# Decoder layer on one core: order of weight splits in the late up chunks, residual rows in two loads, one load later in block 0

## The reference, cut to what matters

```python
x = x + jnp.concatenate([y_mix, y_mem], axis=-1) @ w_out      # (2048, 1536) @ (1536, 1024)
h = rms_norm(x, norm_mlp)
u = jax.nn.relu(h @ w_up)                                     # (2048, 1024) @ (1024, 4096)
x = x + (u * u) @ w_down                                      # (2048, 4096) @ (4096, 1024)
return rms_norm(x, final_norm)
```

## Time and profile before

| what | value |
|---|---|
| median of 3 runs | 2483.25 us (2482.57 to 2483.95) |
| the profiled execution: its own time | 2490.13 us |
| its span, first to last instruction | 2488.3 us |
| PE busy | 2459.6 us (99%) |
| DVE busy | 1869.7 us (75%) |
| ACT busy | 1350.0 us (54%) |
| POOL busy | 344.0 us (14%) |
| mean granted TensorE clock | 0.999 |
| DMA | 411.69 MB, 165 GB/s on the mean |

### The profile page before, as it was taken

One profiled execution on the slowest core, in us unless ns is written; L12 is line 12 of the kernel. 1 busy time (PEld: TensorE's weight loads), 2 busy tenths in 40 slices (PEclk: granted clock), 3 DMA queues, 4 the chain that ended last, 5 costly groups with the idle time before them and its releaser, 6 DMA issues.

```text
span 2488.3 us, 34865 instructions
## 1 busy us (share of the span) xinstructions
PE 2459.6 (99%) x13020; PEld 2125.0 (85%) x13020; DVE 1869.7 (75%) x2779; ACT 1350.0 (54%) x2060; POOL 344.0 (14%) x328
## 2 busy tenths in 40 slices
PE   7999999999999999999999999999999999999998
PEld 7888888888788888888978888898888888889987
DVE  5677468778867887878766778877785677887777
ACT  5544354544554456556655445665565445556655
POOL 0044200000303320000020441000020143000000
PEclk9999999999999999999999999999999999999999
DMA  8422458777842143566552216355664212545555
GB/s 295 169 68 68 163 192 301 256 271 254 281 167 68 52 171 125 174 207 211 199 174 77 76 51 203 110 195 195 210 211 139 84 60 80 192 142 180 186 176 180
DMA packets 236741, 411.69 MB, mean 165 GB/s; under 512 B 10304, under 2 KB 142784, under 8 KB 227616
## 3 DMA queue, kind: packets, MB, share of 16 engines
q1 hardware_dynamic: 235952, 409.20, 48.3%
q10 hardware_dynamic: 624, 0.27, 0.0%
HBM read 365.39 MB, written 44.04 MB: 165 GB/s over the span
## 4 chain that ended last, share of the span: by engine, by line
PE 91%; DVE 4%; DMA 2%; issue 2%; ACT 1%; ACTq 0%; DVEq 0%; POOLq 0%; POOL 0%; SPq 0%
PE banks L2690 27%; PE banks L2692 26%; PE banks L2691 26%; PE banks L2865 3%; DMA raw<-w_mix 1%; DVE w_lo L2497 1%; PE banks L2844 1%; PE banks L2904 1%; PE banks L2908 1%; PE banks L2889 1%; PE banks L2821 1%; DVE u_lo L2408 1%; PE banks L2834 1%; PE banks L2920 1%; DVE c_parts L2541 1%
## 5 line engine op out<-in xcount | busy, mean ns | idle before, releaser
L2690 PE MATMUL banks<-h_hi,w_hi 128*128 128x512 f32 (+1 forms) x1728 | 606.0, 351 | 1.6 <-DVE h_lo L2300 0.7
L2692 PE MATMUL banks<-h_hi,w_lo 128*128 128x512 f32 (+1 forms) x1728 | 598.5, 346 | 0.0
L2691 PE MATMUL banks<-h_lo,w_hi 128*128 128x512 f32 (+1 forms) x1728 | 598.5, 346 | 0.0
L2497 DVE TENSOR_TENSOR w_lo<-raw,w_hi 128x1024 fp32r<-128x1024 f32 (+1 forms) x312 | 366.0, 1190 | 62.1 <-ACT w_hi L1626 61.9
L1626 ACT ACTIVATE w_hi<-raw 128x1024 fp32r<-128x1024 f32 (+1 forms) x312 | 300.5, 1003 | 173.8 <-DMA raw<-w_mix 76.4
L2690 PEld LDWEIGHTS banks<-h_hi,w_hi 128*128 128x128 f32 x1728 | 327.6, 190 | 42.1 <-issue 2.7
L2692 PEld LDWEIGHTS banks<-h_hi,w_lo 128*128 128x128 f32 x1728 | 327.4, 189 | 40.5
L2691 PEld LDWEIGHTS banks<-h_lo,w_hi 128*128 128x128 f32 x1728 | 327.7, 190 | 38.9
L2690 PE MATMUL banks<-w_hi,u_hi 128*128 128x512 f32 x896 | 351.0, 392 | 6.9 <-issue 3.6
L2691 PE MATMUL banks<-w_lo,u_hi 128*128 128x512 f32 x896 | 349.2, 390 | 0.0
L2692 PE MATMUL banks<-w_hi,u_lo 128*128 128x512 f32 x896 | 349.1, 390 | 0.0
(11 more groups left out here) (279 smaller groups left out, 4317.3 us busy)
## 6 DMA issues: line engine op xcount, KB each, us to landing
raw<-w_mix SPq DMA_DIRECT2D x64, 1024.0 KB, 4.8
raw<-in_gla_w_in SPq DMA_DIRECT2D x56, 1024.0 KB, 5.1
raw<-in_w_down SPq DMA_DIRECT2D x48, 1024.0 KB, 5.6
raw<-w_up_mix SPq DMA_DIRECT2D x72, 512.0 KB, 4.7
raw<-in_w_up SPq DMA_DIRECT2D x28, 1024.0 KB, 5.8
raw<-in_w_up SPq DMA_DIRECT2D x36, 512.0 KB, 4.1
raw<-w_out_mix SPq DMA_DIRECT2D x24, 512.0 KB, 4.3
xin<-in_w_down SPq DMA_DIRECT2D x11, 1024.0 KB, 5.0
```

The costliest lines, as they stand in the source:

```text
L2497: nc.vector.tensor_tensor(w_lo[:, i % 2, at], raw[:, i % 2, at], w_hi[:, i % 2, at].bitcast(F32), ALU.subtract).then_inc(lo_split.sem, 1)
L2690: after_chunk(pe.matmul(to, left[0], right[0], start=start, stop=False, skip_group_check=goes_on))
L2691: pe.matmul(to, left[0], right[1], start=False, stop=False, skip_group_check=goes_on)
L2692: return pe.matmul(to, left[1], right[0], start=False, stop=stop, skip_group_check=goes_on)
```

## The change

1. In a late up chunk, ACT splits the weights of up b (both pieces) first, ahead of `late_body` and `corner` of chunk c - 1 and of `keep_part` of M1; before, it did so behind them. DVE takes both pieces of up b's low part first, ahead of `u_sums` of chunk c - 1 and of `add_part` of M2; before, `u_sums` came first and M2's add stood between the two pieces.
2. In blocks 1 to 3 the residual rows come in two loads of 1 MB: tiles 0 and 1 behind chunk C_OUT + 5, tiles 2 and 3 behind chunk C_OUT + 6, with a semaphore of their own, for which DVE waits ahead of M5's add.
3. In block 0 `mix_load(13)` is issued behind the load of step 8 of the MLP and not of step 7.

```diff
+        xres_rest_loaded = Signal(sem("xres_rest_loaded"), 0, 1, 16, 0)
@@ mix_work (SP)
-                        FIRST.mlp + 7: [(mix_load, 13)], FIRST.mlp + 10: [(mix_store, 12)],
+                        FIRST.mlp + 8: [(mix_load, 13)], FIRST.mlp + 10: [(mix_store, 12)],
@@ load_block (SP)
                     if i == C_OUT + (3 if first else 5):
                         sp.wait_ge(*read(n, ("oT", TILES - 1, 1)))
-                        sp.dma_start(xres[:, :, :], x_tiles[:, x_row:x_row + TILES, :])\
+                        tiles = TILES if first else TILES // 2
+                        sp.dma_start(xres[:, 0:tiles, :], x_tiles[:, x_row:x_row + tiles, :])\
                             .then_inc(xres_loaded.sem, 16)
+                    if i == C_OUT + 6 and not first:
+                        sp.dma_start(xres[:, TILES // 2:, :], x_tiles[:, x_row + TILES // 2:x_row + TILES, :])\
+                            .then_inc(xres_rest_loaded.sem, 16)
@@ late_up (ACT)
                     ahead = c - 1 if c % DEPTH else None
+                    late_split_hi(s + 1, 0)
+                    late_split_hi(s + 1, 1)
                     if ahead is not None:
                         late_body(ahead)
                         corner(ahead)
                     keep_part(c, "M1")
-                    late_split_hi(s + 1, 0)
-                    late_split_hi(s + 1, 1)
                     if ahead is not None:
                         u_high(ahead, False)
                     keep_part(c, "M6")
@@ output projection (DVE)
                     next_chunk(C_OUT + 5)
+                    dve.wait_ge(*xres_rest_loaded.at(n, 0))
                     add_product("M5")
@@ late_up (DVE)
                     if LATE_MLP[s - 1][0] == "down":
                         add_down(*LATE_MLP[s - 1][1:])
-                    else:
+                    late_split_lo(s + 1, 0)
+                    late_split_lo(s + 1, 1)
+                    if ahead is not None:
                         u_sums(ahead)
-                    late_split_lo(s + 1, 0)
                     add_part(c, "M2")
-                    late_split_lo(s + 1, 1)
```

## The result

The changed kernel took **2498.04 us** (median of 5 runs, 2497.62 to 2498.77) against 2483.95 (2482.57 to 2486.37) for the kernel before, now with 5 runs: ratio 1.0057, 95% interval 1.0047 to 1.0068. It is slower, by 14.1 us. The forecast was 2499 us, in a range of 2487 to 2511.

The account below looks back on a forecast made before the run. TensorE (PE, busy 99% of the span) was taken as the bound. The terms, +25.1 - 7.0 - 1.65 - 0.3 = +16.1 us, added to the median of 2483.25, gave 2499 us, range 2487 to 2511.

Parts of the forecast that it names:

- Sign, mechanism, place: Late up chunks: slower, chance 0.78, because M6 waits for M1's late keep in 27 chunks that have a chunk ahead.
- Part 1's cost: Late up chunks, new order: 0.93 us of PE wait in each of 27, +25.1 us, bounds +14 to +35.
- keep ends at R + 2.72 + 1.47 = R + 4.19: Late up loop, R the relu's start: the high pieces delay M1's keep by 1.47 us; next relu at R + 11.00.
- One slack: First chunk of a group with a chunk ahead: 0.76 us between M1's keep and M6's start.
- The room on DVE: Late up chunks: M2's add and both u_low end some 0.2 us before M7's add.
- Rival C: Late up chunks: DVE becomes the loop's bound, 1.4 us a chunk, +38 - 9, 2512 us; chance 0.12.
- Part 1's gain: Group starts: the second down chunk's load starts earlier, so four starts lose their waits, -7.0 us, bounds -7.0 and -4.5.
- Part 2: Residual rows at C_OUT + 6, blocks 1 to 3: 1 MB fewer ahead closes PE's gaps, -1.65 us, bounds 0 and -1.65.
- Part 3: Block 0, step 7's load gets another neighbour behind it: -0.3 us, bounds -1.4 and +0.5.
- A: Late up chunks: M1's keep isn't late, so gains stand without the loss, 2474 us; chance 0.12.
- B: Late up chunks: a wash, ACT's pieces pass while it would wait anyway, loss some 0.3 us each, 2482 us; chance 0.08.
- D: Late up chunks: TensorE's clock falls to 1.2 GHz in the 27 chunks, up to +272 us; chance 0.01.

Follow-up runs that it names:

- one_piece: Changed kernel with only the first piece of up b's split ahead of square and sums, the second back behind M1's keep and M2's add: 2487.66 us, ratio 1.0012.
- keep_late: Kernel before with one step moved: ACT makes both high pieces between the corner of c - 1 and M1's keep; DVE's order old: 2504.23 us, ratio 1.0080.
- act_only: Kernel before with ACT's new late-up order and DVE's old one: 2526.26 us, ratio 1.0166.
- keep_order: Kernel before with the new late-up order on ACT and DVE, but M1's keep directly behind the two high pieces: 2479.45 us, ratio 0.9981.
- dve_only: Kernel before with DVE's new late-up order and ACT's old one: 2512.12 us, ratio 1.0110.

## Why the prediction was right, and where its terms were off

*Sign, mechanism, place: right.* M6 waits for M1's keep in 3 chunks x 3 groups x 3 blocks, 27, and nowhere else. The chunks with nothing ahead have none. M6 starts 0.15 behind the keep (0.16 foreseen).

*Part 1's cost: 0.75 us a chunk and not 0.93, 20.5 us in all and not 25.1.* The step that failed is "keep ends at R + 2.72 + 1.47 = R + 4.19". It ends at R + 4.04. From M6's start to the next relu I had 11.00 - 4.35 = 6.65 us, and that holds to 0.01 in every kernel in which M6 is held and DVE keeps up: 4.18 + 6.65 = 10.83 (changed), 3.66 + 6.65 = 10.31 (one_piece), 4.33 + 6.65 = 10.98 (keep_late). keep_late, whose keep has the high pieces directly ahead of it, hits my 4.19 and my 11.00 within 0.02. So the loop was right and the 0.15 are a matter of where the pieces stand. Before, the square starts 0.87 us after the relu whose result it reads, which was at 1140.08 (timeline of ACT, kernel before):
```profile
1140.95 0.84 ACT L1675 ACTIVATE u_parts<-u_parts 128x768 f32<-128x768 f32 x1
```
With the pieces between them, the first piece starts at + 0.75 (1131.55) and the square doesn't wait for the relu any more. The pieces fill a pause of 0.12, which leaves 0.03 open. One slack was read too large: the prediction took 0.76 for the first chunk of all nine groups, but in block 3, chunk 5, M6 had started 0.28 earlier, and that is the 0.28 more.

*The room on DVE: right.* I had 0.2 us between u_low and M7's add. In the changed kernel's timeline of DVE, block 1, chunk 10:
```profile
1138.12 1.22 DVE L2414 TENSOR_TENSOR u_lo<-u_parts,u_hi 128x1024 fp32r<-128x1024 f32 x1 [0.57 <-ACT u_hi L1592]
1139.57 0.42 DVE L2547 TENSOR_TENSOR c_parts<-banks,c_parts 128x256 f32<-128x256 f32 x1 [0.23 <-PE banks L2698]
```
DVE waits 0.23 for M7. Rival C needs that to be used up, as act_only does.

*Part 1's gain: 5.0 us and not 7.0.* All the waits went, as I said: the load is now issued 7.11 us ahead of the next relu and not 3.90, 3.2 us sooner where I had 3.4. But 7.0 was what one execution had lost. keep_order, which has this gain and no loss, is 5 us faster than the kernel before. The step was taking for the kernel rather than for an execution that stood 6.9 us above the median, which was itself the hint.

*Part 2: 0.6 and not 1.65*, for the same reason; the extra wait costs nothing, as foreseen. *Part 3: 0 and not 0.3.*

*Sum:* 20.5 - 5.0 - 0.6 = 14.9 us, against 14.1 measured between the medians. The forecast was 16.1: a cost too high by 4.6 less gains too high by 3.3. That the time was met to 1 us is in part luck: these errors cancel.

*The rivals.* A needed a keep in time, and the keep came 1.3 us later. B was right in that something of the pieces' time passes in a pause, but it is 0.12 us and not 0.6. D: with its 27 waits, the changed kernel shows no fall of the clock ahead of its last matmul. The rival wasn't empty, though: in act_only the clock did fall once, for 3.4 us behind a wait of 2.65, and cost about 1.5 us. The Trainium skill's case of short, frequent waits between groups of matmuls that let the clock swing ("TensorE: Matmul & The Clock Gate", "A second HAM failure mode: psum-queue depth-cycling") isn't met by the changed kernel; act_only's single fall is the nearest to it that these traces show.

## What to carry to other kernels

When work is moved ahead on an engine, list every instruction that it passes and ask of each which engine stands behind it: here the square and the sums could come 1.7 us later for nothing, while a keep of 0.37 us between them was the one step that TensorE waited for, and moving that one step turned + 14 us into - 5. If the side work is a loop, go once round it from one mark (relu to keep, keep to matmul, matmul to relu): one sum then gives the period of every variant in which the same link holds the loop (10.31, 10.83 and 10.98 here, not the 11.59 and 11.43 of act_only and dve_only). And price waits for loads from more than one profile: one that stands well above the median of the runs, as here by 6.9 us, may hold more of them than the kernel has on average.

## What was not expected of the hardware

Two profiles of the same kernel, medians 0.06% apart, lost 7.0 and 2.2 us at the same loads: ACT's wait for the same 1 MB was 2.39 us in one and 0.57 in the other, with the load issued at the same distance from the relu. On ACT the square, which reads the result of the relu just ahead of it and waits for its semaphore, started 0.12 us later behind it (0.87 against 0.75) than the independent first piece did, so the pieces between the two were partly free. And one wait of 2.65 us in act_only was followed by 3.4 us at TensorE's lower clock, while waits of 2.28 and 1.92 us and the 27 short ones of the changed kernel weren't.
